# Expert-row stores one tile later, lower-row gathers ahead of the last store, and a reordered list of weight chunks between two layers

## What is computed

```
def grouped_moe(h, router_w, router_bias, w_gate, w_up, w_down):
    ...
    out = jnp.zeros_like(h)
    for e in range(N_EXPERTS):
        y = (jax.nn.silu(h @ w_gate[e]) * (h @ w_up[e])) @ w_down[e]
        out = out + gates[:, e:e + 1].astype(h.dtype) * y
    return out

def reference(...):
    for l in range(DEPTH):
        mod_l = (silu_c @ ada_w[l] + ada_b[l]).reshape(bsz, 1, N_MOD, d)
        ...
        x_l = x_l + g1_l * y_l                          # mixer
        h_l = modulate(rmsnorm(x_l, norm_ffn_g[l]), sh2_l, sc2_l)
        ...
        x_c = x_c + g2_c * f[:bsz * c_len].reshape(bsz, c_len, d)
        x_l = x_l + g2_l * f[bsz * c_len:].reshape(bsz, s_len, d)
    return rmsnorm(x_l, final_norm_g)
```

## Time and profile before

| what | before |
|---|---|
| three runs, median | 960.75 us |
| the profiled execution, its own time | 957.07 us |
| span in its profile, first to last instruction | 955.3 us |
| PE busy, DVE busy, ACT busy, POOL busy | 85%, 47%, 28%, 20% of the span |
| mean granted clock of TensorE | 0.941 of full |
| HBM read, written | 297.38 MB, 14.20 MB |

### The profile page before, as it was taken

How to read it: one execution, slowest core, us unless ns; L and a number is a source line. 1 busy time by engine, 2 the same in 40 slices (tenths; PEclk the granted TensorE clock), 3 DMA queues, 4 the chain that set the end, 5 groups by cost and what they waited for, 6 DMA issues and landing times.

```text
span 955.3 us, 31672 instructions
## 1 busy us (share of the span) xinstructions
PE 807.3 (85%) x13340; PEld 542.0 (57%) x13341; DVE 449.5 (47%) x1101; ACT 265.1 (28%) x464; POOL 193.3 (20%) x365
## 2 busy tenths in 40 slices
PE   3799999999969898989888639999977785676895
PEld 2444444444458686868667525458445663565774
DVE  2379999944574344444333261665264221121232
ACT  2313536331412222222222130256032120111222
POOL 2300000010043334443424400000005121111220
PEclk9999999999979999999999959999998997787998
DMA  9992398568489999999999982881665999999992
GB/s 347 355 384 103 131 378 306 177 241 307 171 302 369 416 399 416 409 414 413 410 416 408 384 327 108 292 324 67 261 239 215 406 410 419 427 423 422 422 419 102
DMA packets 70694, 309.03 MB, mean 324 GB/s; under 512 B 9753, under 2 KB 10193, under 8 KB 54257
## 3 DMA queue, kind: packets, MB, share of 16 engines
q1 hardware_dynamic: 54608, 275.78, 73.1%
q0 software_dynamic: 15040, 30.22, 8.8%
q10 hardware_dynamic: 992, 2.26, 0.6%
HBM read 297.38 MB, written 14.20 MB: 326 GB/s over the span
## 4 chain that ended last, share of the span: by engine, by line
DMA 50%; PE 25%; DVE 18%; issue 3%; SPq 2%; ACT 2%; POOL 0%; DVEq 0%; POOLq 0%; ACTq 0%
DMA weight_ring<-in_exp_w_down 10%; DMA weight_ring<-in_exp_w_up 10%; DMA weight_ring<-in_exp_w_gate 10%; DVE arena L1069 9%; PE ps L609 7%; DMA arena<-in_exp_w_up 7%; DMA hT<-in_exp_w_down 5%; DMA arena<-in_exp_w_gate 4%; PE ps L875 3%; PE ps L832 3%; DMA weight_ring<-in_ev_w_in 2%; PE ps L575 2%; SPq L371 2%; PE ps L776 2%; PE ps L915 1%
## 5 line engine op out<-in xcount | busy, mean ns | idle before, releaser
L776 PE MATMUL ps<-weight_ring,arena 128*32 128x128 f32 x5760 | 185.6, 292 | 45.9 <-DMA weight_ring<-in_exp_w_up 28.1
L776 PEld LDWEIGHTS ps<-weight_ring,arena 128*32 128x32 f32 x5760 | 175.8, 119 | 60.0 <-DMA weight_ring<-in_exp_w_up 26.8
L1374 DVE TENSOR_TENSOR arena<-arena,ps 128x64 f32<-128x64 f32 x128 | 28.3, 221 | 228.4 <-ACT arena L1758 228.3
L1758 ACT ACTIVATE arena<-ps 128x64 f32<-128x64 f32 x128 | 28.7, 224 | 358.2 <-PE ps L776 358.2
L575 PE MATMUL ps<-hT,weight_ring 128*128 128x512 f32 x256 | 114.7, 604 | 2.4 <-DMA weight_ring<-in_ev_w_in 2.1
L1069 DVE SCALAR_TENSOR_TENSOR arena<-arena,par 128x512 f32<-128x512 f32 x132 | 94.8, 749 | 4.0 <-DVE arena L1100 0.8
L786 PE MATMUL ps<-weight_ring,arena 128*32 128x256 f32 x1440 | 92.6, 382 | 1.5 <-DMA weight_ring<-in_exp_w_down 0.9
L776 PE MATMUL ps<-arena 128*32 128x128 f32 x2432 | 75.2, 283 | 17.2 <-DMA arena<-in_exp_w_up 14.3
L575 PEld LDWEIGHTS ps<-hT,weight_ring 128*128 128x128 f32 x256 | 48.3, 192 | 66.8 <-issue 62.7
L776 PEld LDWEIGHTS ps<-arena 128*32 128x32 f32 x2432 | 72.0, 115 | 21.6 <-issue 19.2
L1758 ACT ACT_TABLE_LOAD x64 | 82.1, 1283 | 6.3 <-DVEq L1333 1.2
(11 more groups left out here) (324 smaller groups left out, 866.6 us busy)
## 6 DMA issues: line engine op xcount, KB each, us to landing
weight_ring<-in_ada_w SPq DMA_DIRECT2D x24, 2048.0 KB, 14.3
weight_ring<-in_exp_w_gate SPq DMA_DIRECT2D x22, 2048.0 KB, 10.0
weight_ring<-in_exp_w_up SPq DMA_DIRECT2D x22, 2048.0 KB, 10.4
weight_ring<-in_exp_w_down SPq DMA_DIRECT2D x22, 2048.0 KB, 10.9
arena<-in_exp_w_gate SPq DMA_DIRECT2D x10, 2048.0 KB
hT<-in_exp_w_down SPq DMA_DIRECT2D x10, 2048.0 KB, 11.1
arena<-in_exp_w_up SPq DMA_DIRECT2D x10, 2048.0 KB
weight_ring<-in_ev_w_in SPq DMA_DIRECT2D x4, 2048.0 KB, 19.6
```

The lines of the kernel that those rows point to most:

```text
L776: last = mm(ps[32 * qd:32 * qd + 32, 1 + hh, 0:P].rearrange("p (m n) -> p m n", m=2), xgT[:, MT * k:MT * k + MT], w2[:, k, :, at:at + 64], ...
L1758: s.activation(act_sl[:, 64 * hh:64 * hh + 64], ps[:, 1 + hh, 0:64], ACT.Silu).then_inc(s_sl[l], 1)
```

## The change

POOL stores tile k-1, not k, in the step of tile k, after the copy and the gather of that step; the last tile is stored by a call of its own. The lower-row gathers 0 and 1 are issued ahead of that last store, 2 and 3 behind it. `MID` puts `("qkv", 0, 2)` first (slot 5), then four `ada` chunks; SP's wait stands before the fourth chunk in place of the fifth, and is for upper-row gather 1 in place of 3. `GAP_ADA` is 2: PE makes two `ada` products in the gap, and one each behind the third and fourth key/value tile (before: three, and one behind the third).

```
-GAP_ADA = 3
-MID = (_ada(1, 6, 9) + [("qkv", 0, 2), ("qkv", 0, 0)] + _ada(1, 9, 10) +
-       [("qkv", 0, 1), ("out1", 0, 0), ("out1", 0, 1)] + _ada(1, 10, 12))
+GAP_ADA = 2
+MID = ([("qkv", 0, 2)] + _ada(1, 6, 10) + [("qkv", 0, 0), ("qkv", 0, 1), ("out1", 0, 0), ("out1", 0, 1)] +
+       _ada(1, 10, 12))
-USE = [0, 1, 2, 3, 5, 4] + list(range(6, len(MID)))
-MID_SLOT = [3, 4, 5, 0, 2, 1, 3, 0, 1, 4, 5]
+USE = [1, 2, 0] + list(range(3, len(MID)))
+MID_SLOT = [5, 3, 4, 0, 1, 2, 3, 0, 1, 4, 5]
@@ SP
                 if sum(count) - sum(pre_n) == GAP_ADA + 1:
-                    sp.wait_ge(s_yg[NT - 1], 16)
+                    sp.wait_ge(s_yg[1], 16)
@@ PE
-                if t == 2:
-                    ada_product(7)
+                if t >= CT:
+                    ada_product((7, 5)[t - CT])
@@ PE
                 if un == 1:
-                    pe.wait_ge(s_red, state["ada"] - 1)
-                if un == 3:
                     pe.wait_ge(s_red, state["ada"])
@@ DVE
-                if t == 2:
-                    read_columns(7)
+                if t >= CT:
+                    read_columns((7, 5)[t - CT])
@@ POOL
+                def store(k, u):
+                    pool.wait_ge(s_y[0], k + 2)
+                    pool.sem_inc(s_pool, 1)
+                    g.dma_start(places[k], y_sb[u]).then_inc(s_yo[u], 16)
...
-                            pool.wait_ge(s_y[0], k + 2)
-                            pool.sem_inc(s_pool, 1)
-                            g.dma_start(places[k], y_sb[u]).then_inc(s_yo[u], 16)
+                            if u or not isinstance(j, int):
+                                store(k - 1, (u - 1) % AHEAD)
...
-                    expert_rows(total)
+                    expert_rows(total, lambda: store(rounds * AHEAD - 1, AHEAD - 1))
...
-            def expert_rows(total):
-
-                below = pool.value_load(ctl[0:1, 2, E - 2:E - 1], min_val=1, max_val=MAXTILES)
-                for c, end, done in ((1, below, [s_ym] * NT), (0, total, s_yg)):
+            def expert_rows(total, store_last):
+
+                def rows_in(c, i, done):
+                    g.indirect_dma_start(yg[:, c, i, :], None, y_dram,
+                                         bass.IndirectOffsetOnAxis(row_i[:, c, i:i + 1], 0)).then_inc(done, 16)
+
+                def stored(end):
                     for u in range(AHEAD):
                         pool.wait_ge(s_yo[u], ((end + (AHEAD - 1 - u)) >> 2) * 16)
                     pool.sem_inc(s_pool, 1)
-                    for i in range(NT):
-                        g.indirect_dma_start(yg[:, c, i, :], None, y_dram,
-                                             bass.IndirectOffsetOnAxis(row_i[:, c, i:i + 1], 0)).then_inc(done[i], 16)
+
+                stored(pool.value_load(ctl[0:1, 2, E - 2:E - 1], min_val=1, max_val=MAXTILES))
+                for i in range(NT):
+                    if i == CT:
+                        store_last()
+                    rows_in(1, i, s_ym)
+                stored(total)
+                for i in range(NT):
+                    rows_in(0, i, s_yg[i])
```

## The result

The changed kernel takes **964.84 us** (median of 22 runs, 961.51 to 969.98), the kernel before, measured beside it, 961.49 (22 runs): ratio 1.0033, interval 1.0023 to 1.0044, so some 3.2 us slower. The forecast was 962.5 us, +1.8, with a range to 964.2.

What follows compares the result with a forecast made beforehand. DMA weight loads bound the expert stages, single waits the gap, then PE. The gap's -0.1 and the moved product's +1.9 gave +1.8 us on 960.75, so 962.5, range 959.4 to 964.2 (its own case 961.6 to 963.6).

Steps and rivals of the forecast that it cites:

- the baseline: Starting time of the sum: 957.07 us profiled, median 3.7 higher, so 960.75 plus the forecast 1.8.
- the -0.1 of the gap: Last expert weights to PE's transposes: they start at 566.0 instead of 566.07, a gain of 0.1 us.
- the first of part 1: Layer-0 expert stage: POOL's stores one tile later cost and win nothing, since weights decide.
- Part 1, the order at the end: End of expert stage: first lower gather issued near 535.7, 4.8 us earlier; last store 538.4; fourth gather about 540.9.
- Part 2, the third load: Gap: second product hangs on the third load, slowed by gathers to 552.4, so transposes start at 566.0.
- The lower rows: Gap: the fourth lower-row gather lands at 550.4 instead of 554.7, 4.3 us earlier.
- some 4: Gap: DVE idles some 4 us between first and second lower add, waiting to read the second product.
- the bound of 547.2: Gap: earliest landing of the third load, if gathers cost it nothing; the other bound was 553.4.
- Part 3: Behind the fourth key/value tile: the product moved out of the gap adds 1.88 us in full.
- the upper rows: Upper-row gathers go out from about 547.0, 1 us later; the third is in by 561, at no cost.
- The rivals: Four: equal turns +1.2 us (0.15), loads not slowed -0.9 (0.20), faster -2.9 (0.14), upper rows late +3.2 (0.06).
- the faster rival: Gap: lower rows land at 550.4, third load no later than 547.5; 2.9 us faster, 957.9; chance 0.14.

Runs made afterwards that it cites:

- the record: The first measurement of the change, with one profile per kernel: profiled before 957.07 us, median 960.75; profiled changed kernel 961.72, median 964.84, ratio 1.0033.
- set 4: Before, the whole change and each half run together, before's median 957.00 us: before 1.0001, changed 1.0016, chunk part only 0.9986, POOL part only 0.9988.
- the nine profiles with the longer tile: Changed kernel and its variants in the record and sets 2, 3 and 5, all with later loop store and chunk part: 5.95 us a tile instead of 5.44.
- set 5: Before, chunk part only, and the changed kernel with a later DVE read, before's median 961.50 us: 0.9997, 1.0010 and 1.0020.
- the chunks alone: Against before, only the new load order, SP's wait and the moved PE product, POOL's code as before: 0.9972, 0.9986 and 1.0010 in sets 1, 4 and 5.
- the changed kernel with the late read: Against the changed kernel, DVE reads the gap's second product behind all four lower adds: 1.0020 to before, in set 5 (median 964.10 us).
- POOL's part alone: Against before, only stores one tile later and lower rows around the last store, loads and products as before: 0.9973 in set 1, 0.9988 in set 4.
- sets 1 and 3: Set 1: before, each half, later loop stores alone, before's median 957.18 us, ratios 0.9972 to 1.0000. Set 3: variants of the changed kernel, before's median 961.52.
- 2 and 4: Set 2: changed kernel again and small variants, before's median 961.01 us, changed 1.0027. Set 4: before, changed and both halves, before's median 957.00, changed 1.0016.

## Why the prediction was wrong

Its direction had the second chance (slower 0.41, within 0.2% 0.45), its time was 2.3 us short and its range ended 0.6 us below the result. Of the 2.3 us, 0.7 is the baseline: the three runs it started from had a median of 960.75, the 22 beside the changed kernel 961.49. By the ratio the change cost 3.2 us where 1.8 was forecast, and taken as a difference the range ended at +3.4. That the direction came out is partly luck: the product that moved costs its 1.9 us here too (603.75), but the -0.1 of the gap was summed for a situation that the record's execution never met.

- **The step that failed** is the first of part 1: "Inside the DMA-bound stage this costs nothing and wins nothing: 40 stores stay 40 stores, and weights decide." It holds in set 4 to about 1 us: last write 249.1 us behind the first, before 247.9. In the record's profile it does not. There, from first to last write, the changed kernel takes 252.2 us. Over the nine profiles with the longer tile it is 251.3 to 259.0 (252.1 in set 5), while before and the chunks alone take 248.0 and 245.5 where they have the stop too: at least 3 us more. The share of tiles that have slack is smaller than I took it for. Of 39 distances between writes, 7 are above 8 us in before of sets 4 and 5 (waits for weights; 6 in the record's) and 5 in eight of the nine, so the longer tiles eat up part of those waits and the rest shows at the end.
- **The baseline.** The prediction noted that "the median of the runs stands 3.7 higher" than the profiled execution and added it as a constant. It was a sign: the profile has no stop, as those of the kind at 957, and the three timed runs are of the kind at 961. The sum was made for one and compared with the other.
- **Where this time went.** Part comes back in the gap. From the last write to the transposes it is 28.5 us in before of set 5, and 20.1 and 20.9 in the changed kernels: most of the copies and loads that the gap waited for were ready. The product behind the fourth tile (594.80 and 603.75, 1.9 us each) costs its forecast 1.9. The first query product over all nine changed kernels of this kind stands at 607.6 in the mean (605.6 to 612.6), 0.9 behind before's 606.7 in set 5. Before's profiled execution there was itself 2.9 above its median, the nine on average 1.0 above theirs. That makes 0.9 + 2.9 - 1.0 = 2.8 of the 3.2 us, but it is the mean of nine against one, and the nine scatter over 7 us at this mark; the split between stage and gap is therefore an estimate. Nor do the times show that the longer tile makes the whole loss: in set 5 the chunks alone, with a tile of 5.44, stand at 1.0010 and the changed kernel with the late read at 1.0020, with intervals that overlap. Part of the loss is that the gap's gain of the chunk part does not arrive in this kind.
- **Part 1, the order at the end:** right. In set 4 the lower gathers went out at 537.39, 538.89, 542.68 and 543.97 with the last store at 541.61 (forecast 535.7 to 540.9; the last write starts 3.3 us later in that execution than in the record's before).
- **Part 2, the third load:** right in kind, and in size for the load, as set 4 shows (552.78; 566.13). The lower rows were not: they landed at 552.6 where 550.4 was forecast, so the pause was 2.52 us where "some 4" was forecast. (The lower end of its own range, +0.8, doesn't follow from the bound of 547.2 that it names.) The chunk, however, was said to leave "which relieves only what stands behind the third". That was wrong: the gathers themselves stand there. Alone, the chunk part brings the fourth lower row from 10.38 to 6.54 us. In the sum this changed nothing, because with POOL's part the second product, behind the third load, ends last.
- **Gap against the same set:** the forecast was a gain of 0.1. Against before of set 4 (568.2) it was 2.1, and the query product came 0.8 us earlier, not 1.8 later. The time was still 1.5 us longer (interval 0 to 3). What is lost behind the query product, in set 4 by the two parts alone as well (3.0 and 3.4 us won there, 1.3 and 1.1 in the time by the ratios), was not found.
- **Part 3 and the upper rows:** right in effect; the second product took 1.89 us and DVE waited for an upper row in none of the twenty profiles, though in set 4 they went out from 549.49 and not from 547.0.
- **The rivals.** None of the four is what happened; all sit in the gap. What the faster rival says of the third load ("no later than 547.5") is what the chunks alone do.

What stays open: what holds PE's release for some 5 us at the loop's entry and again behind the loop, and what decides whether a set of runs has it (sets 1 and 3 ran on a chip of the same number, 12, and so did 2 and 4 on number 8, one of each kind); why the loop with the later store then runs at 5.95 us; how POOL's part alone fares there; and whether the late read helps where there is no stop.

No kernel here is faster than before in both kinds. The chunks alone come nearest: 0.9972 and 0.9986 without the stop, 1.0010 [0.9999, 1.0020] with it.

## What to carry to other kernels

Where a profiled execution stands further from the median than runs scatter (3.7 us here, with runs within 0.6), find out where the difference sits before summing anything on that profile. An edit to an engine's order inside a loop of 40 rounds isn't free because a transfer bounds the loop: with 0.5 us more in a round the stage took at least 3 us longer. Two edits that shorten the same gap must be tried one by one: each alone won 0.1 to 0.3%, together they did not, and in set 4's gap the reason in sight is that the earlier gathers push the third load to where the second product waits for it. And where a wait is put down to nobody, ask the program which semaphore it is for and who else waits for it: here that moved the stop from VectorE to TensorE's release.

## What was not expected of the hardware

- The program before, unchanged, has two medians, 957 and 961.5 us, and all profiles of each of the five sets were of one kind. The profiles of the slower kind have a stop of 4.00 to 4.13 us (1.37 in one) at the entry of the first expert loop: a semaphore that a finished matmul should raise is raised 5.1 to 5.7 us late (2.7 in that one), and again some us late behind the loop, for instance 7.6 in the chunks alone.
- A loop can hold two periods, 5.44 and 5.95 us, and keep one for all of its tiles that do not wait for weights. Neither one nor 48 instructions more ahead of it changed that.
- A load of 2 MB that shares the queues with row gathers landed 25.95 us after its issue instead of 22.0, and a row gather of 512 KB 6.54 instead of 10.38 us once the load beside it was gone.
